# Down projections with the low and the high part of the hidden tiles in one row, and one 512-column product over both

## What is computed

```python
def swiglu(x, w_gate, w_up, w_down):
    return (jax.nn.silu(x @ w_gate) * (x @ w_up)) @ w_down
# D_MODEL = 1024, D_FF = 2816, SEQ = 256
h = h + FFN_RES * g1[:, None, :] * swiglu(u, w_ff1_gate[l], w_ff1_up[l], w_ff1_down[l])   # first block, twice
x = x + 0.5 * swiglu_2(rms_norm(x, ffn1_norm[l]), ffn1_w_in[l], ffn1_w_out[l])            # second block, four times
```

## Time and profile before

| | |
|---|---|
| runs, us | 1640.9, 1642.5, 1642.66 |
| median, us | 1642.5 |
| span of the profiled execution, us | 1640.7 |
| products of down projections | 3168 (1056 on each of L1747, L1748, L1749) |
| residual updates, L1359 | 48, mean 484 ns |
| TensorE busy | 1616.5 us, 99% of the span |

### The profile page before, as it was taken

The page is one execution under the profiler, slowest core; times in us unless marked ns, Lnnn a source line. Parts: engine busy times, 40 slices in busy tenths (PEclk is TensorE's granted clock), DMA queues, the critical chain, the costliest instruction groups (busy, mean ns, idle before and its releaser), DMA issues.

```text
span 1640.7 us, 33817 instructions
## 1 busy us (share of the span) xinstructions
PE 1616.5 (99%) x13617; PEld 1579.3 (96%) x13617; DVE 1154.1 (70%) x1452; ACT 799.1 (49%) x973; POOL 171.4 (10%) x193
## 2 busy tenths in 40 slices
PE   6999999999999999999999999999999999999999
PEld 4999999999999999999999999999999999999999
DVE  6877789778766657666688876656665588776653
ACT  3444445355544455444565654445444465554432
POOL 1100114500000000000052200000000035200000
PEclk9999999999999999999999999999999999999999
DMA  9998897646666467665744566568665764456653
GB/s 332 303 315 250 250 329 229 221 147 189 183 190 184 135 193 203 187 169 159 231 134 129 152 179 183 154 180 217 193 181 149 204 186 129 129 162 191 170 159 114
DMA packets 501553, 315.62 MB, mean 192 GB/s; under 512 B 14815, under 2 KB 489674, under 8 KB 501450
## 3 DMA queue, kind: packets, MB, share of 16 engines
q1 hardware_dynamic: 491824, 282.33, 60.5%
q0 software_dynamic: 8496, 29.92, 5.2%
q10 hardware_dynamic: 1130, 1.90, 0.3%
HBM read 313.04 MB, written 1.05 MB: 191 GB/s over the span
## 4 chain that ended last, share of the span: by engine, by line
PE 71%; DVE 4%; ACT 2%; issue 1%; ACTq 0%; DVEq 0%
PE accs L1747 20%; PE accs L1749 20%; PE accs L1748 19%; PE wide L1787 1%; PE accs L1787 1%; PE accs L1785 1%; PE wide L1785 1%; PE accs L1786 1%; PE wide L1786 1%; DVE wlo L1060 1%; PE wide L2018 1%; PE accs L1845 1%; PE accs L1847 0%; PE accs L1846 0%; PE ps_score L2067 0%
## 5 line engine op out<-in xcount | busy, mean ns | idle before, releaser
L1747 PE MATMUL accs<-uhi_shift,whi 128*128 128x256 f32 x2304 | 650.8, 282 | 3.0 <-DVE ulo L1111 1.2
L1749 PE MATMUL accs<-uhi_shift,wlo 128*128 128x256 f32 x2304 | 645.8, 280 | 0.0
L1748 PE MATMUL accs<-ulo,whi 128*128 128x256 f32 x2304 | 643.2, 279 | 0.0
L746 ACT CAST whi<-raw 128x2048 fp32r<-128x2048 f32 (+2 forms) x294 | 499.5, 1702 | 101.4 <-PE accs L1749 61.9
L1060 DVE TENSOR_TENSOR wlo<-raw,whi 128x2048 fp32r<-128x2048 f32 (+2 forms) x249 | 496.3, 2001 | 4.5 <-ACT gat L987 3.1
L1747 PEld LDWEIGHTS accs<-uhi_shift,whi 128*128 128x128 f32 x2304 | 433.4, 188 | 11.3 <-issue 5.2
L1748 PEld LDWEIGHTS accs<-ulo,whi 128*128 128x128 f32 x2304 | 434.3, 188 | 1.2 <-issue 1.2
L1749 PEld LDWEIGHTS accs<-uhi_shift,wlo 128*128 128x128 f32 x2304 | 433.2, 188 | 0.0
L1747 PE MATMUL accs<-hhi,whi 128*128 128x256 f32 x1056 | 297.6, 282 | 0.7 <-DVE wlo L1060 0.7
L1748 PE MATMUL accs<-hlo,whi 128*128 128x256 f32 x1056 | 298.0, 282 | 0.0
L1749 PE MATMUL accs<-hhi,wlo 128*128 128x256 f32 x1056 | 296.3, 281 | 0.0
(11 more groups left out here) (368 smaller groups left out, 2258.7 us busy)
## 6 DMA issues: line engine op xcount, KB each, us to landing
raw<-in_ffn_w_in SPq DMA_DIRECT2D x176, 512.0 KB, 5.1
in_turn<-in_w_ada POOLq DMA_DIRECT2D x56, 512.0 KB, 5.5
raw<-in_w_mix_in SPq DMA_DIRECT2D x52, 512.0 KB, 4.7
raw<-in_ffn_w_out SPq DMA_DIRECT2D x64, 384.0 KB, 3.6
raw<-in_w_ff_gate SPq DMA_DIRECT2D x44, 512.0 KB, 5.0
raw<-in_w_ff_up SPq DMA_DIRECT2D x44, 512.0 KB, 6.3
raw<-in_w_in SPq DMA_DIRECT2D x40, 512.0 KB, 5.0
raw<-in_ffn_w_out SPq DMA_DIRECT2D x64, 320.0 KB, 4.0
```

The lines of the kernel that those rows point to most:

```text
L746: nc.scalar.copy(whi[:, n % RING, 0:cols], raw[:, n % RING, 0:cols]).then_inc(hi_ready, 1)
L1747: mm(dst, wh, xh, start=first, stop=False)
L1748: mm(dst, wh, xl, start=False, stop=False)
L1749: return mm(dst, wl, xh, start=False, stop=last)
```

## The change

`hlo` and `hhi` become one tensor, `h_parts`: for each hidden tile 256 columns of the low part, then 256 of the high part. For each hidden tile the kernel now issues two products instead of three: the high weights by all 512 columns of the row, into the whole bank (low part's share in columns 0 to 255, high part's in 256 to 511), and the low weights by the 256 high columns, into the bank's upper half. The two halves of the bank are then added to the residual by two updates on VectorE, one behind the other; the second waits for the first (`half_added`), and it is the second that signals `evacuated`. Nothing else is changed.

```diff
-        hhi = hidden.enter_context(nc.sbuf_tensor("hhi", [P, KF, T + 2], F32R))[:, :, 0:T]
-        hlo = hidden.enter_context(nc.sbuf_tensor("hlo", [P, KF, T], F32R))
+        h_parts = hidden.enter_context(nc.sbuf_tensor("h_parts", [P, KF, 2 * T + 2], F32R))
+        hlo, hhi = h_parts[:, :, 0:T], h_parts[:, :, T:2 * T]
...
                         dve.wait_ge(chunk_used, it * RING + RING + n0 + t + 1)
+                        nc.vector.scalar_tensor_tensor(out=hm, in0=acc[(e0 + m) % 2][:, T:2 * T], scalar=gm, in1=hm,
+                                                       op0=ALU.mult, op1=ALU.add).then_inc(half_added, 1)
+                        dve.wait_ge(half_added, it * 2 + KD * i + m + 1)
                         nc.vector.scalar_tensor_tensor(out=hm, in0=acc[(e0 + m) % 2][:, 0:T], scalar=gm, in1=hm,
                                                        op0=ALU.mult, op1=ALU.add).then_inc(evacuated, 1)
...
                         kk = side * (KF // 2) + k
-                        ins = three(acc[(e0 + m) % 2][:, 0:T], vh[:, k], vl[:, k], hhi[:, kk], hlo[:, kk],
-                                    kk == 0, kk == KF - 1)
+                        dst = acc[(e0 + m) % 2]
+                        mm(dst, vh[:, k], h_parts[:, kk, 0:2 * T], start=kk == 0, stop=False)
+                        ins = mm(dst[:, T:2 * T], vl[:, k], hhi[:, kk], start=False, stop=kk == KF - 1)
                     ins.then_inc(chunk_used, 1)
```

## The result

| | before | after |
|---|---|---|
| runs, us | 1640.9 to 1642.66 (4 runs) | 1651.4, 1652.95, 1653.07, 1653.78 |
| median, us | 1642.22 | 1653.01 |
| ratio, 95% interval | | 1.0065 (1.0053 to 1.0076) |
| span of the profiled execution, us | 1640.7 | 1649.7 |

The changed kernel is slower by 10.8 us on the medians and by 9.0 us on the profiled spans. The two differ because the profiled execution of the changed kernel is its shortest (1651.4 us, mean granted clock 1.000); the other three took 1.6 to 2.4 us more, at 0.998 or 0.999. The forecast was 1644.6, with a range up to 1651.0: the result lies 2.0 us above that range.

The account below looks back on a forecast made before the run. TensorE's product pitch plus stalls was taken as the bound. Terms summed to -0.7 us at 216 ns and +5.0 at 225, middle +2.1: span 1642.8, plus 1.8 for the median, 1644.6 us; range 1638.5 to 1651.

Parts of the forecast that it names:

- The pitch of the 512-column product: TensorE's time per fp32r product of 512 columns: 216 to 225 ns, middle 220.5, making a chunk 3.73 us against 3.91.
- 23 pairs: Chunk pairs in the loops of down1 to down4, ruled by VectorE's chain: 3.9 / 6.2 us more at 216 / 225 ns.
- down0: Layer where VectorE is the limit and one pair holds 16 small products: 0.3 / 0.8 us more at 216 / 225 ns.
- down5: Layer without `ulo`, its split still early, so all 16 chunks gain: 3.7 / 2.1 us less at 216 / 225 ns.
- behind down0 and down1: Layer borders where TensorE waits for a crowded VectorE: 0.5 us more behind each, the one behind down0 an estimate.
- low end: 512-column pitch of 216 ns on TensorE: the columns hide the weight load, as in float32 rows; 1641.8 us, no change.
- high end: 512-column pitch on TensorE if the excess goes with the columns: 2 x 118.5 = 237 ns, nothing saved.
- The chain through VectorE: Last product, update, `uhi`, `ulo`, split: second update adds 0.53 us, split done at 4.29 instead of 3.76 us.
- The restart: TensorE after a late split: starts 0.05 us later, and its second product stands 0.10 us further behind the first.
- slack: In a down3 pair, the split was said to end 0.26 us before TensorE wants its result.
- The chain does not bind: Rival: TensorE's gain shows in all layers, 17 us less (13 to 22), some 1627 us; chance 0.1.
- The 512-column product is no cheaper than two of 256: Rival: 237 ns, about 11 us more, 1653 us; chance 0.13 for pitch above 227 or more lateness than counted.

Follow-up runs that it names:

- small step: Kernel before, with a clear of eight unused columns and a wait for it ahead of VectorE's one update: 1643.43 us, ratio 1.0005.
- one-update kernel: Changed kernel with only the upper half's residual update, the low part's share left out of the output: 1640.07 us, ratio 0.9983.
- split first: Changed kernel with VectorE's split moved ahead of the wait for TensorE and the two updates: 1634.40 us, ratio 0.9957; run again 1635.05 us, ratio 0.9956.
- split-first move in the kernel before: Kernel before, with VectorE's split moved ahead of the wait for TensorE: 1637.47 us, ratio 0.9975.
- without pads: Changed kernel, h_parts rows every 2048 bytes instead of 2056: with the split ahead 1633.09 us, again 1633.63 us; without that move 1652.61 us.
- study of pitches: Changed kernel with rows of fp32r products behind its end, from h_parts rows or 2048-byte stretches: 512 columns took 234 and 227 ns a product.

## Why the prediction was wrong, point by point

- **The pitch of the 512-column product. This is the step that failed.** The prediction took 216 to 225 ns, middle 220.5. It is 233. With that, a chunk is 11 x 351 = 3.86 us, not 3.73, and TensorE gains 0.05 us a chunk instead of 0.18. Put into the recorded sum, 233 ns gives 8.0 (23 pairs of 8.19, less 0.04 in six of them) + 0 (last pairs) - 0.45 (first pairs) + 1.2 (down0) - 0.9 (down5) + 0.5 (end) + 1.0 (behind down0 and down1) = some 9.3 us (9.6 with the prediction's own 118.5 ns beside it); the trace has +9.0. So one mis-sized term makes the miss on the span. The median is 1.8 us further up still, with the lower mean clock of three of the four executions; the sum had no term for that.
- **Why it failed.** Three parts add up to the 12.5 ns. 4.5 come from the middle between 216 and 225: the low end rested on the float32 rows, which show "no excess at 512", but take two clock periods a column. They were no measure for fp32r, whose stretches have a fixed excess of 13 to 14 ns at 256 and at 512 columns. 2 are what those stretches take beyond 225. The last 6 are the rows of `h_parts`, which no row of the trace before could show. That the high end of 237 came nearer, by doubling the 256-column product, is in part luck: from the stretches doubling gives 240, against 227.
- **The Trainium skill** ("TensorE: Matmul & The Clock Gate", Back-to-back issue gap) gives 215.8 ns for 512 columns by its formula N / 2.4 + 2.5, which it calls the gap of an isolated product, and about 131 ns for a stream of products with their weight loads. The products here, a stream with loads, take 233, or 227 from the stretches; neither figure is met, and the measurement decides for this type.
- **The chain through VectorE: right, step by step.** Updates 0.53 us apart were foreseen, 0.52 measured; a split ending 4.29 us after the last product was foreseen and is there. The three old products with two updates, and the new ones with one, separate it cleanly: the first has the lateness without the product, the second the product without the lateness.
- **The restart: right.** 0.05 + 0.10 us were foreseen; TensorE starts 0.06 us behind the split's end (1092.51 to 1092.57), and its next start is 0.33 behind instead of 0.23. But the slack was told as 0.26 us, measured to the moment when TensorE wants the weights. A wait that actually takes hold costs the restart as well, so the pair lengthens from some 0.12 us on. The small step shows it (up to 7.89 us a pair with 0.14 us). The sum had the restart in it; the sentence on the slack hadn't.
- **down0, down5, the end, the borders.** At 233 ns: 1.2 foreseen, 1.2 measured; -0.9 and -0.9; 0.5 and 0.5; behind down1 0.5 and 0.5, behind down0 0.5 and 0.3. In down0 the agreement is in part luck: the pairs with a sum of squares take 8.04 us, not 8.2, and the pair with the small products is 0.8 longer, not 0.5. The pairs in down5 are 7.72 us (22 x 0.351), not 7.4 to 7.6, by the pitch alone; the last two take 8.4 and 8.6, before the change 8.5 and 8.7.
- **The clock: right, but read from a row that can't show it.** "Full clock" was taken from the slices of the page, which read 9 throughout. They do so in the one-update kernel too, where the clock was 0.5 for nearly 7 us: a slice is 41 us long. The stretch behind the small products settles it for the kernel before (granted clock 1.00, third number from the end):

```profile
208.00:212.00 4.00, 4.00 (x36) 4.00 (x36) 2.63 (x4) 1.16 (x1) 1.05 (x2) 1.00 1.00 301
```

- **The rivals.** "The 512-column product is no cheaper than two of 256" came nearest: 233 against its 237 ns, 9.0 us on the span against its 11. That its 1653 us equals the measured median is luck: the change cost 1.8 us more on the medians than on the spans. It had less than 0.13 and the range ended 2 us short of it. "The chain does not bind" is refuted. That TensorE gained in full with the split first (1634 us) doesn't speak for it, since the order on VectorE had to be changed for that.
- **A miss of the experiments.** The split-first move in the kernel before was expected to do nothing, since its pairs have no gap. The pairs had none, and yet it gained 4.7 us, most of it at the layers' borders. The wait at 636.54 was in the earlier trace rows, read only as a place where 0.5 us would be added, never as one where VectorE's list could be put in a better order.

**What stays open.** Why the clock falls behind the small products of down0 in some executions and not in others: it did so in the profiles of the one-update kernel, of the small step, of two kernels without pads and of the study, with waits of 0.60 to 1.84 us ahead of it, and it didn't in the seven others, one of them the changed kernel itself with 1.40 us. No run took the late transfer or the small products away. What makes one row of `h_parts` slower than another, and why the pitch without pads is 230 ns in some layers and 236 in others. And whether the rows without pads are worth anything on the median (1.4 us, within the intervals). The best of these kernels, split first without pads, took 1633.1 and 1633.6 us, some 9 us less than the kernel before, of which 4.7 come from the move alone in the old kernel.

## What to carry to other kernels

Fewer and longer products save only what they do save in the same number type. Take the cost of a new length from rows of the same type, once with a fixed excess and once scaled by columns, and keep both as ends; a row of another type shouldn't pull the middle. Better still, measure the length from the very tensor that will be read: here its rows alone added 6 ns. Before a vector instruction is added, follow the chain from the last product to the next thing that TensorE waits for, and count its slack including the restart, which a hidden wait doesn't pay and a late one does. If that chain has work in it that doesn't depend on its beginning (here the split), putting that work ahead is worth trying first, and the end of each layer is worth the same look.

## What the runs showed of the hardware

- A 512-column fp32r product took 233 ns from the rows of `h_parts` (2056 bytes apart) and 227 from stretches of 2048 bytes, at a granted clock of 1.00, where the columns alone would be 213. At 256 columns it was 118 and 120, where the columns would be 107. Weights of 32 or 64 columns instead of 128 change nothing in it. With 2 or 128 columns a product takes 111 to 112 ns, as the one-column products with 128x128 weights in the earlier trace rows.
- The pitch depends on the row that is read: 226 to 243 ns among the rows of `h_parts` in the study, the same for a row each time within 2 ns.
- The granted clock fell to 0.5 (1.2 GHz) among products of one or two columns, in the study of pitches while TensorE was issuing without a gap. In these stretches of the study (columns as above), products of 128 columns fill the first line until 1685.0; then come the 28 of two columns, of which the first eight lie before the fall, and from 1690.2 on products of 512 columns.

```profile
1682.00:1686.00 4.00, 4.00 (x38) 4.00 (x37) 0.00 (x0) 0.00 (x0) 0.00 (x0) 0.98 0.00 0
1686.00:1696.00 10.00, 10.00 (x35) 6.54 (x35) 0.00 (x0) 0.00 (x0) 0.00 (x0) 0.50 0.00 0
```

Ahead of the fall a two-column product took 112 ns, behind it 213; the 512-column products that followed took 427 ns until the clock rose at 1696.1. In down0 the clock fell behind the 16 one-column products in five of the profiled executions and stayed at 1.00 in the others, among them the kernel before after a wait of 0.47 us.
